# One pair of heads prepared in the stage before, a second one early, and both scan directions inverted in lockstep

## The chip, the cores and the metric

The kernel runs on one core of one Trainium2 chip. The metric is the time of one execution on the device in microseconds (us). Three runs of the kernel before gave 1978.81, 1972.71 and 1967.83 us, so its median is 1972.71 us.

## What is computed

One inference step of a two-layer flow-matching backbone with 1024 channels. There are 384 tokens: 128 context tokens and 256 latent tokens on a grid 64 wide. Everything is in 32-bit floats. Each layer does this:

```python
h = rmsnorm(x) * (1 + sc1) + sh1                   # sc, sh, gt: "modulation", silu(cond) @ ada_w + ada_b
x = x + 0.5 * gt1 * (silu(h @ Wg) * (h @ Wu)) @ Wo # feed-forward, 2816 hidden
p = (rmsnorm(x) * (1 + sc2) + sh2) @ mix_w_in      # one projection for three mixers
o = concat(gla(p_gla), hyena(p_hy), rwkv7(p_rw))   # 6 heads | FFT long convolution | 6 heads
x = x + gt2 * (o @ mix_w_out)
x = x + 0.5 * gt3 * feed_forward(...)
```

The RWKV-7 mixer runs in both directions along the tokens. For each head and direction the state follows `state = state * w_t + (state @ a_t) b_t^T + v_t k_t^T`, and the output is `state @ r_t`. GLA is a chunked gated linear attention, also in both directions. The final states of the context tokens are outputs too.

## The kernel before

Tokens lie along the free dimension and channels on the 128 partitions. A program (`with nc.Block()`) is written per stage and runs one instruction list per engine, in exactly the order in which the Python calls it; there is no planner. Semaphores order the engines: each `..._step` raises one, each `after_...` waits for it. A wait blocks everything behind it on its engine. The stages of a layer are `ffn_stage`, `mix_in_stage`, `mixers_stage` and a second `ffn_stage`.

`mix_in_stage` makes the 13 units of `mix_w_in`, each 48 products of 128x386 in three passes, streamed through two weight slots, and computes the Hyena mixer beside them. `mixers_stage` does GLA and RWKV-7. RWKV's six heads go as three pairs, called A, B and C (pairs 0, 1 and 2); one head sits on partitions 0 to 63 and the other on 64 to 127 (`half(e)`). The methods of class `Pair` are the steps of a pair:

- Preparation: low-rank products (`pe_low`), sigmoids, decay sums by a scan (`dve_decay_sums`), unit keys with their root, inverse and spread (`pe_gate_norm`, `pe_spread_k`), then gate, turned values and bonus, the decayed keys (`dve_decayed`, 5 instructions per direction), the products `nat` and six `gram` products.
- Inverse: in 64-token chunks a triangular matrix is inverted by powers, in ten dependent steps s1, s2, s2q, s3, s4, s5, s6, s7, s8, s9. In the kernel before each step is a call per direction z, for example `pe_s4(pe, 0)` and `pe_s4(pe, 1)`. `each` issues 12 products of 64x64, alternating between the array's quadrant for head 0 (partitions 0 to 63 in and out) and the one for head 1. A product appears as two MATMUL instructions in the trace. PE's result of a direction is evicted by ACT or DVE (`act_inverse`, `dve_power_q`, `dve_q`, `dve_y`), and then that direction's next product may start.
- Scan: four dependent steps of `x`, `u`, `state` and `out`, then a normalisation (`pe_mean`, `pe_var`, `pe_spread_v`, `dve_out`).

Each pair holds three PSUM banks for itself and shares bank 6; bank 7 is for the modulation. Pair C reuses the memory and the banks of pair A and so is begun when A's output is written (`after_first_pair`). Pair B uses GLA's banks and is begun when GLA ends (`after_gla`). The order in `mixers_stage` is: A's preparation and inverse beside GLA, then A's scan beside B's preparation, then B's inverse beside C's preparation, C's inverse beside B's first scan steps, and both scans.

Between these steps PE works through `ada(pe, s, kt)`: products with the modulation weights, 32 units of 1 MB in layer 0 and 16 in layer 1. They are loaded through two slots in the first half of the stage and three in the second (`ADAS`), by the SP queue.

Of the kernel before, what the change touches and what calls it, by code (L numbers as in the profile page):

```python
# [24 lines left out]
TOK = CTX + LAT  # L25
KT = D_MODEL // 128
C = 64
# [80 lines left out]
def build(nc, x_in, cond, ada_w, ada_b, w1_in, w1_out, mix_in, mix_out, w2_in, w2_out, gains, final_gain, chan, lowrank_a,  # L108
# [15 lines left out]
    with stack:  # L124
# [287 lines left out]

        class Place:
# [4 lines left out]
            def __init__(self, at):  # L418
                self.at = at

            def __call__(self, name, shape, dt=F32):
                names[0] += 1
# [683 lines left out]
        def mix_in_stage(lay, P, PR, TG, AL, MO, buffers, following):  # L1106
# [5 lines left out]
            MIX = Steps(" ".join(f"m{i}_s m{i}" for i in range(N_TILES - N_PLAIN)) + " al_g al_s al")  # L1112
# [7 lines left out]
            with ExitStack() as scope, nc.Block() as block:  # L1120
# [7 lines left out]
                HC = sb(scope, "hyena_const", [128, NHCONST])  # L1128
                HW = sb(scope, "hyena_w", [128, 640])
                UC = sb(scope, "conv", [128, 6, W386])  # L1130
# [4 lines left out]
                XALR = flat_zt[0:32, 0:PADT]  # L1135
                RN = UC[0:HY_HID, 5, 0:TOK]
# [25 lines left out]
                def _(act):  # L1162
# [18 lines left out]
                    for n, u in enumerate(UNITS):  # L1181
# [15 lines left out]
                        if n == 10:  # L1197
# [6 lines left out]
                def _(dve):  # L1204
# [4 lines left out]
                    def tap(i, name, at):  # L1209
                        row = P[:, T_HY + i, at:at + W386]  # L1210
                        if at == 1:
                            op = nc.vector.tensor_scalar(UC[:, i, :], row, chn("conv_w", 6 + i), chn("conv_b", i), ALU.mult, ALU.add)
                        else:
                            op = nc.vector.scalar_tensor_tensor(UC[:, i, :], row, chn("conv_w", 6 * at + i), UC[:, i, :], ALU.mult, ALU.add)
# [60 lines left out]
                    def hyena_out():  # L1275
# [6 lines left out]
                        for ct in range(2):  # L1282
                            for (a, b), x0 in zip(SEGS, seg2(UC[:, ct, :])):
# [39 lines left out]
                    for n in range(N_MIX):  # L1323
# [9 lines left out]
                        if n == 4:  # L1333
                            wait_own("e5")
                            nc.vector.tensor_tensor(Z[:, :, :], UC[:, 2:4, :], UC[:, 4:6, :], ALU.mult).then_inc(hdve_done, DV.step("z"))
                        if n in (9, 10):
                            spectrum(n - 9)
                        if N_HY + 1 <= n <= N_MIXED:
                            dve.wait_ge(pb_done, n)
                            for t in range(2):  # L1340
                                i = 2 * (n - 1 - N_HY) + t
                                if i:
                                    dve.wait_ge(mix_done, 2 * i)
                                shift_mix(dve, PR[:, i, :], 128, i, SH[:, :], SHT[:, :], PR[:, i, 0:TOK], mix_done, MIX, f"m{i}")
                        if n == 11:
                            low_rank_input()
                        if n == 12:
                            hyena_out()
                            evict(n)

                @block.tensor
                def _(pe):
# [55 lines left out]
                    for n, u in enumerate(UNITS):  # L1408
# [36 lines left out]
        class Pair:  # L1445
# [3 lines left out]

            def __init__(self, place, sems, lay, pr, banks, shared, PR, TG, AL, MO, shared_free=None):  # L1450
# [5 lines left out]
                self.PE = Steps("loww low g kk vt kspread bonus nat0 nat1 gram00 gram01 gram02 gram10 gram11 gram12 " +  # L1456
                                " ".join(f"s{i}_{z}" for i in ("1", "2") for z in z2) + " s2q_0 s2q_1 s3_0 s3q_0 s3_1 s3q_1 " +
                                " ".join(f"s{i}_{z}" for i in ("4", "5", "6", "7", "8", "9") for z in z2) + " " +
                                " ".join(f"x{t} u{t} s{t} o{t}" for t in range(3)) + " x3 u3 o3 mu var vspread")
                self.AC = Steps("kx2 sigw siga kt g kstd vt e1 e2 first bt00 bt01 bt02 bt10 bt11 bt12 " +  # L1460
                                " ".join(f"s{i}_{z}" for i in (1, 2, 3, 5, 6) for z in z2) + " u0 u1 u2 u3 o sq std")
                self.DV = Steps("st_init kfloor km rk cum kinv kk bn bon bl ab0 ab1 r d0 et0 d1 et1 mr00 mr01 mr02 mr10 mr11 mr12 " +
                                " ".join(f"s{i}_{z}" for i in ("1", "2q", "3q", "4", "7", "8", "9") for z in z2) + " " +
                                " ".join(f"x{t} u{t} sum{t} st{t}" for t in range(3)) + " x3 u3 oc og vinv on out")
                self.PL = Steps("identity decay q0 q1")
# [1683 lines left out]
```

## Time and profile before

| | us |
|---|---|
| median of three runs | 1972.71 |
| the profiled execution | 1975.78 |
| its span, first to last instruction | 1974.0 |
| PE busy | 1885.5 (96%) |
| DVE busy | 1092.9 (55%) |
| ACT busy | 744.2 (38%) |
| POOL busy | 32.1 (2%) |
| mean granted PE clock | 0.986 of full speed |

PE is TensorE, PEld its weight loads, DVE is VectorE, ACT is ScalarE, POOL is GpSimd, SP issues the DMAs. Matmuls overlap in the pipeline, so PE's busy time is a union of modelled spans. The stretches in the rows below were cut where PE's instructions show a step begin: the mixers' stage of layer 0 runs from 472.45 to 700.87, that of layer 1 from 1429.40 to 1649.17.

### The profile page before, as it was taken

What the parts mean: (1) busy time and instruction counts of PE and PEld (TensorE: products, weight loads), DVE (VectorE), ACT (ScalarE), POOL (GpSimd) and SP (SyncE); (2) the same over time, 40 slices, a digit from 0 to 9 for tenths busy, and PEclk for the clock granted to TensorE, in tenths of its full rate; (3) what the DMA queues carried; (4) which work ended last, traced back from release to release, by engine and by line L of the source; (5) the groups of instructions that cost most, each with busy time, mean ns of one, the idle gap of its engine ahead of it and who ended that gap; (6) DMA issues with size and microseconds to landing.
All of it is one profiled execution on the core that took longest, in us unless ns stands there. A gap on an engine that the chain in (4) does not pass through costs nothing. (4 is left out here: it accounts for less than half of the span.)

```text
span 1974.0 us, 38649 instructions
## 1 busy us (share of the span) xinstructions
PE 1885.5 (96%) x16410; PEld 1739.0 (88%) x16410; DVE 1092.9 (55%) x1853; ACT 744.2 (38%) x1117; POOL 32.1 (2%) x64
## 2 busy tenths in 40 slices
PE   5999999998889999999999999999978899999998
PEld 3988999996666789999999999999947688999997
DVE  3544444865766475555455554477576746655533
ACT  3333333345334254333343333344363324433322
POOL 0000000000001000000000000000000100000000
PEclk9999999998999999999999999999989999999999
DMA  7766233423446343332343333342241412333332
GB/s 280 275 221 220 103 119 136 176 86 93 129 152 219 115 147 128 127 123 100 132 147 128 127 116 108 127 187 95 78 131 49 130 50 87 128 117 119 106 132 91
DMA packets 73335, 263.25 MB, mean 133 GB/s; under 512 B 9712, under 2 KB 11120, under 8 KB 57072
## 3 DMA queue, kind: packets, MB, share of 16 engines
q1 hardware_dynamic: 73200, 261.27, 39.0%
q8 instruction: 107, 1.75, 0.4%
q14 instruction: 28, 0.23, 0.0%
HBM read 259.08 MB, written 2.16 MB: 132 GB/s over the span
## 5 line engine op out<-in xcount | busy, mean ns | idle before, releaser
L160 PE MATMUL ps<-h_head,w_head 128*128 128x386 f32 x1824 | 623.5, 342 | 4.1 <-ACT h_head L293 2.1
L160 PE MATMUL ps<-h_head,w_rest 128*128 128x386 f32 x1824 | 619.3, 340 | 0.0
L160 PE MATMUL ps<-h_rest,w_head 128*128 128x386 f32 x1824 | 617.3, 339 | 0.0
L223 ACT ACTIVATE w_head<-w_raw 128x2048 fp32r<-128x2048 f32 (+1 forms) x176 | 303.0, 1722 | 606.0 <-PE ps L160 588.8
L226 DVE TENSOR_TENSOR w_rest<-w_raw,w_head 128x2048 fp32r<-128x2048 f32 (+1 forms) x176 | 360.6, 2049 | 209.3 <-ACT w_head L223 209.3
L160 PEld LDWEIGHTS ps<-h_head,w_head 128*128 128x128 f32 x1824 | 345.8, 190 | 23.1 <-issue 16.9
L160 PEld LDWEIGHTS ps<-h_head,w_rest 128*128 128x128 f32 x1824 | 345.9, 190 | 0.0
L160 PEld LDWEIGHTS ps<-h_rest,w_head 128*128 128x128 f32 x1824 | 343.0, 188 | 0.2
L160 PE MATMUL ps<-gu_head,w_head 128*128 128x384 f32 x832 | 278.4, 335 | 0.1
L160 PE MATMUL ps<-gu_head,w_rest 128*128 128x384 f32 x832 | 277.7, 334 | 0.0
L160 PE MATMUL ps<-gu_rest,w_head 128*128 128x384 f32 x832 | 277.7, 334 | 0.0
L405 DVE TENSOR_TENSOR gate_in<-ps,rstd_all 128x386 f32<-128x386 f32 x88 | 49.2, 559 | 199.8 <-PE ps L160 199.7
L160 PEld LDWEIGHTS ps<-gu_head,w_head 128*128 128x128 f32 x832 | 156.0, 188 | 1.4 <-issue 0.4
L160 PEld LDWEIGHTS ps<-gu_rest,w_head 128*128 128x128 f32 x832 | 156.0, 188 | 0.1
L160 PEld LDWEIGHTS ps<-gu_head,w_rest 128*128 128x128 f32 x832 | 156.2, 188 | 0.0
L823 ACT ACTIVATE gu_head<-gu 128x384 f32 (+1 forms) x88 | 46.2, 526 | 198.5 <-DVE gu L934 198.5
L686 DVE SCALAR_TENSOR_TENSOR x<-ps,gate,x 128x128 f32<-128x128 f32 (+1 forms) x96 | 34.9, 412 | 107.1 <-PE ps L160 107.1
L939 DVE TENSOR_TENSOR gu_rest<-gu,gu_head 128x384 f32 (+1 forms) x88 | 49.2, 559 | 63.7 <-ACT gu_head L823 63.7
L820 ACT ACTIVATE silu<-gate_in 128x128 f32<-128x128 f32 (+1 forms) x176 | 69.2, 440 | 10.8 <-DVE gate_in L405 10.8
L934 DVE SCALAR_TENSOR_TENSOR gu<-up_in,silu 128x128 f32<-128x128 f32 (+1 forms) x176 | 65.2, 412 | 1.6 <-ACT silu L820 1.6
L160 PE MATMUL ps<-ar_identity,bk 64*64 64x64 f32 (+1 forms) x576 | 46.2, 293 | 17.6 <-ACT bk_tok L1810 12.9
L160 PEld LDWEIGHTS ps<-ar_identity,bk 64*64 64x64 f32 (+1 forms) x576 | 34.0, 168 | 32.4 <-ACT bk_tok L1810 21.7
(300 smaller groups left out, 1784.2 us busy)
## 6 DMA issues: line engine op xcount, KB each, us to landing
w_raw<-in_w_in SPq DMA_DIRECT2D x88, 1024.0 KB, 4.8
w_raw<-in_w_out SPq DMA_DIRECT2D x64, 704.0 KB, 4.1
w_raw<-in_ada_w SPq DMA_DIRECT2D x41, 1024.0 KB, 6.3
ada_raw<-in_ada_w SPq DMA_DIRECT2D x31, 1024.0 KB, 6.3
w_raw<-in_mix_in SPq DMA_DIRECT2D x26, 1024.0 KB, 4.8
w_raw<-in_mix_out SPq DMA_DIRECT2D x8, 1024.0 KB, 5.0
hyena_const<-in_hconst SPq DMA_DIRECT2D x2, 1792.0 KB, 9.4
x<-in_x_in SPq DMA_DIRECT2D x1, 1536.0 KB, 12.1
```

The costliest lines, as they stand in the source:

```text
L160: return nc.tensor.matmul(out, lhsT, rhs, start=start, stop=stop)
L223: return nc.scalar.activation(self.HI[src], self.RAW[src], ACT.Copy)
L226: return nc.vector.tensor_tensor(self.LO[src], self.RAW[src], self.HI[src].bitcast(F32), ALU.subtract)
L405: return nc.vector.tensor_tensor(out, bank(b, WIDE), self.ALL[:, :], ALU.mult)
L686: last = nc.vector.scalar_tensor_tensor(xs, psum[:, a:b], g, xs, ALU.mult, ALU.add)
L820: last_silu = nc.scalar.activation(SIL[:, j, a:b], GRAW[:, j, a:b], ACT.Silu, bias=GRAW[:, j, TOK + s:TOK + s + 1])
L823: nc.scalar.activation(GHI[:, ds(k * 2 + j, 1), :].rearrange("p o t -> p (o t)"), GU[:, j, :], ACT.Copy)\
L934: last_gu = nc.vector.scalar_tensor_tensor(GU[:, j, a:b], URAW[:, j, a:b], URAW[:, j, TOK + s:TOK + s + 1], SIL[:, j, a:b], ALU.add, ALU.mult)
L939: nc.vector.tensor_tensor(GLO[g].rearrange("p o t -> p (o t)"), GU[:, j, :], GHI[g].rearrange("p o t -> p (o t)").bitcast(F32), ALU.subtract)\
```

## The change

**Preparation of pair A in the stage before.** `mix_in_stage` gets A and calls its first part between its last units. The rest of A's preparation (gate, turned values, bonus, decayed keys, nat, gram) stays in `mixers_stage`.

```diff
@@ mix_in_stage, ACT, unit loop
+                        if n == 10:
+                            A.act_square(act)
+                            A.act_decay_rates(act, 0)
+                            A.act_decay_rates(act, 1)
                         evict(n, u)
+                        if n == 10:
+                            A.act_key_rate(act)
+                            A.act_key_factor(act)
+                            A.act_decays(act)
+                            A.act_key_root(act)
...
-                        if n == 10:
+                        if n == 9:
                             wg = T_WG - N_PLAIN
@@ DVE
+                        if n == 6:
+                            low_rank_input()
                         if n == 11:
-                            low_rank_input()
+                            A.dve_decay_sums(dve)
+                            A.dve_keys(dve)
+                            A.dve_key_floor(dve)
                         if n == 12:
+                            A.dve_key_inverse(dve)
                             hyena_out()
+                            A.dve_unit_keys(dve)
+                            A.dve_rates(dve)
                             evict(n)
@@ PE
                             signal_back()
+                            pe.wait_ge(low_done, 1)
+                            A.pe_decay_rank(pe, 0)
+                            A.pe_decay_rank(pe, 1)
...
+                                if (n, t, kt) == (11, 0, 5):
+                                    A.pe_key_rank(pe)
+                                if (n, t, kt) == (11, 1, 0):
+                                    A.pe_norm(pe)
+                                if (n, t, kt) == (12, 0, 6):
+                                    A.pe_spread_k(pe)
```

Buffers get new addresses for this (`Homes`), so that A's tiles, and later C's, do not overlap what is still in use.

**Pair C early on one bank.** C's low-rank products, sums and unit keys run through bank 6 alone during A's scan, beside B's preparation. Its gate, values, bonus, decayed keys, nat and gram follow after A's end.

```diff
+                        C.in_banks(6, 6, 6, 6)
+                        after_first_inverse(pe)
+                        C.pe_decay_rank(pe, 0)
...
+                        after_first_pair(pe)
+                        C.in_banks(0, 1, 2, 0)
+                        C.pe_gate(pe)
+                        C.pe_turn_v(pe)
+                        C.pe_bonus(pe)
```

**Lockstep on four quadrants.** A step of the inverse is now one call for both directions. It issues 24 products in which direction 0 uses the quadrants (0 to 0) and (1 to 1) and direction 1 uses (0 to 1) and (1 to 0), and it waits for the evictions of both directions first. Because direction 1's result lands in the other half of the partitions, its steps on DVE that combine it with data in the old half are written as two instructions over 64 partitions (in `dve_nat` the off-diagonal part, in `dve_power_q`, `dve_q` and `dve_y` all of direction 1), and so is its `pool_q`.

```diff
+            def pe_s4(self, pe):
+                self.both(pe, self.after_act, "s3")
+                self.both(pe, self.after_dve, "s3q")
+                self.each(self.second_banks(), self.of(self.D8, self.far), self.q_far, "s4", (0, 0))
...
+            def each(...):
+                for c in range(NCH):
+                    for e in range(2):
+                        for z in range(2):
+                            last = mm(bank(banks[z], TOK)[half(to[z] ^ e), c * C:c * C + C], lhsT(z, c, e), rhs(z, c, e))
...
@@ dve_y
+                if z == 0:
+                    last = nc.vector.tensor_tensor(self.Y[:, 0, :, :], self.XQ[:, 0, :, 1, :], product, ALU.add)
+                else:
+                    for e in range(2):
+                        last = nc.vector.tensor_tensor(self.Y[half(e), 1, :, :], self.QB[half(e)], product[half(1 - e)], ALU.add)
```

**New orders.** Each engine's list in `mixers_stage` is rewritten, one list for layer 0 and one for layer 1. In PE's list for layer 0 the part that follows A's end now alternates B's inverse with C's gram, and C's inverse with B's last inverse steps and B's scan:

```diff
+                        B.pe_s1(pe)
+                        ada(pe, 2, 5)
+                        C.pe_gram(pe, 0, 0)
+                        B.pe_s2(pe)
+                        C.pe_gram(pe, 0, 1)
+                        B.pe_s2q(pe)
...
+                        C.pe_s1(pe)
+                        B.pe_s789(pe, 7)
+                        ada(pe, 3, 1)
+                        C.pe_s2(pe)
+                        B.pe_s789(pe, 8)
+                        C.pe_s2q(pe)
+                        B.pe_s789(pe, 9)
```

The `ada` units are spread anew: in layer 0, units 7 to 12 now stand in A's inverse where one stood before. All of them go through two slots; the three-slot second half is gone, and SP's list loads units 2 to 15, then 16 to 19 after GLA, then 20 to 31 after A's end, with the state loads and stores between.

## Rows read from the trace of the kernel before

**Rows 1.** First line of the page.

```profile
span 1974.0 us, 38649 instructions
```

**Rows 2.** Busy by stretch: length, PE, PEld, DVE, ACT, POOL, clock, DMA share, GB/s.

```profile
472.45:521.21 48.76, 38.55 (x456) 20.59 (x456) 32.18 (x59) 30.19 (x42) 6.03 (x11) 0.82 0.44 134
521.21:557.53 36.32, 33.63 (x912) 30.59 (x909) 22.97 (x72) 7.57 (x13) 0.00 (x0) 1.00 0.30 92
557.53:602.38 44.85, 39.51 (x613) 24.19 (x611) 29.02 (x65) 23.32 (x46) 6.37 (x12) 1.00 0.66 205
602.38:667.38 65.00, 62.48 (x1527) 51.81 (x1523) 38.08 (x76) 19.10 (x42) 2.56 (x6) 1.00 0.45 141
667.38:700.87 33.49, 29.87 (x535) 20.54 (x531) 15.53 (x43) 8.02 (x25) 0.00 (x0) 1.00 0.61 194
1429.40:1476.32 46.92, 35.75 (x455) 20.12 (x456) 32.37 (x59) 30.07 (x42) 5.93 (x11) 0.89 0.46 140
1476.32:1513.33 37.01, 33.81 (x904) 31.79 (x901) 22.97 (x73) 7.57 (x13) 0.00 (x0) 0.95 0.21 62
1513.33:1557.84 44.51, 35.36 (x553) 25.01 (x551) 29.16 (x65) 22.84 (x45) 6.49 (x12) 0.92 0.15 40
1557.84:1619.54 61.70, 60.27 (x1511) 51.29 (x1507) 37.74 (x75) 18.83 (x41) 2.56 (x6) 1.00 0.35 115
1619.54:1649.17 29.63, 26.44 (x478) 21.73 (x479) 15.74 (x44) 7.81 (x26) 0.00 (x0) 0.88 0.03 6
385.00:470.50 85.50, 85.50 (x473) 82.53 (x471) 54.56 (x92) 32.07 (x48) 0.00 (x0) 1.00 0.26 87
```

**Rows 3.** Timeline of PE in the first inverse: start, us, instruction.

```profile
516.05 2.75 PE L160 MATMUL ps<-mixer_out,k_tok 64*32 64x64 f32 x144
...
518.73 0.92 PE L160 MATMUL ps<-ar_identity,bk 64*128 64x192 f32 x8
...
527.25 2.82 PE L160 MATMUL ps<-power_and_q,decay_inv 64*64 64x128 f32 x48
...
543.39 3.01 PE L160 MATMUL ps<-decay_in,chunk_start_state 32*64 32x64 f32 x144
...
546.33 1.61 PE L160 MATMUL ps<-power,decay_incl 64*64 64x64 f32 x48
...
547.88 1.06 PE L160 MATMUL ps<-w_raw,cond_silu 128*32 128x512 f32 x8
```

**Rows 4.** Timeline of DVE and ACT in the first inverse.

```profile
524.27 0.49 ACT L1816 ACTIVATE decay_inv<-ps 128x384 f32<-128x384 f32 x1 [0.91 <-PE ps L160]
...
530.38 0.34 DVE L1941 TENSOR_TENSOR power_and_q<-power_and_q,ps 128x192 f32<-128x192 f32 x1
...
532.57 0.54 DVE L1846 TENSOR_TENSOR power_and_q<-power_and_q,ps 128x384 f32<-128x384 f32 x1
```

**Rows 5.** Timeline of DVE in the mixers' opening, layer 0.

```profile
476.04 1.67 DVE L2248 TENSOR_SCALAR decay_in<-ps,chan 128x386 f32<-128x386 f32 x3 [2.97 <-PE ps L160]
...
482.47 0.95 DVE L1863 TENSOR_TENSOR_SCAN cum<-const,sig_w 128x384 f32<-128x384 f32 x1
...
489.92 2.06 DVE L1896 TENSOR_TENSOR bk<-power_and_q,decay_inv 64x384 f32<-64x384 f32 x4
...
498.70 2.62 DVE L2254 SCALAR_TENSOR_TENSOR decay_in<-decay_in,exp 128x772 f32<-128x772 f32 x2
```

**Rows 6.** Timeline of ACT and PE in the opening, layers 0 and 1.

```profile
493.14 0.83 ACT L2199 ACTIVATE exp<-exp 64x772 f32<-64x772 f32 x1
...
475.93 3.64 PE L160 MATMUL ps<-w_raw,cond_silu 128*32 128x512 f32 x16
...
1431.69 1.92 PE L160 MATMUL ps<-w_raw,cond_silu 128*32 128x512 f32 x16
```

**Rows 7.** PE at the start of pair 1: three low-rank products' first two.

```profile
558.75 0.91 PE L160 MATMUL ps<-p_rwkv,lowrank_w 32*128 32x384 f32 x4
```

**Rows 8.** DMA issues of the modulation weights: count, KB each, median us to landing.

```profile
w_raw<-in_ada_w SPq DMA_DIRECT2D x41, 1024.0 KB, 6.3
```

More of the change, by code:

```diff
@@ L1445, in build @@
         class Pair:
+            EARLY = ("loww0 loww low kk kspread".split(), "kx2 sig0 sigw siga kt e1 e2 kstd".split(), "cum km rk kfloor kinv kk bn".split())
             def __init__(self, place, sems, lay, pr, banks, shared, PR, TG, AL, MO, shared_free=None):
@@ new lines, in both, with near, far, of @@
+            def both(self, pe, after, *names):
+                for name in names:
+                    for z in range(2):
+                        after(pe, f"{name}{z}" if name == "q" else f"{name}_{z}")
+            def near(self, z, e):
+                return half(e)
+            def far(self, z, e):
+                return half(e ^ z)
+            def of(self, buf, side):
+                return lambda z, c, e: buf[side(z, e), z, c, :]
+            def power(self, side):
+                return lambda z, c, e: self.XQ[side(z, e), z, c, 0, :]
@@ L1946, in dve_q @@
                 self.after_pe(dve, f"s{i}_{z}")
-                self.tt(self.XQ[:, z, :, 1, :], self.XQ[:, z, :, 1, :], bank(bb, TOK).rearrange("p (c t) -> p c t", t=C), ALU.add, f"s{i}_{z}")
+                product = bank(bb, TOK).rearrange("p (c t) -> p c t", t=C)
+                if z == 0:
+                    last = nc.vector.tensor_tensor(self.XQ[:, 0, :, 1, :], self.XQ[:, 0, :, 1, :], product, ALU.add)
+                else:
+                    old, new = (self.QB, self.XQ[:, 1, :, 1, :]) if i == "3q" else (self.XQ[:, 1, :, 1, :], self.QB)
+                    for e in range(2):
+                        last = nc.vector.tensor_tensor(new[half(e)], old[half(1 - e)], product[half(e)], ALU.add)
+                self.dve_step(last, f"s{i}_{z}")
             def dve_y(self, dve, i, z):
@@ new lines, in mixers_stage @@
+                LEFT, RIGHT = Place(homes.above), Place(homes.right_at)
+                G = Gla(Place(0, decay_in=LEFT, exp=LEFT, exp_cum=LEFT, exp_minus_cum=LEFT, cum=LEFT, std=LEFT, chunk_start_state=RIGHT, score=RIGHT, k_tok=RIGHT),
+                        SEMS[5:10], lay, (3, 4, 5), P, MO)
+                row_at = LEFT.at
+                mod_row = LEFT("mod_row", [128, 1, 2, ADA_W // 2])
+                A.begin_late(SEMS[0:5])
+                A.in_banks(0, 1, 2, 6)
+                late_at = homes.outer().at
@@ new lines, in mixers_stage @@
+                assert homes.ceiling <= nc.sbuf_top and LEFT.at <= homes.early_at and RIGHT.at <= late_at
+                B_ROWS, B_LEFT, B_RIGHT = Place(homes.rows_at), Place(homes.above), Place(homes.right_at)
+                B = Pair(Place(0, gram=B_ROWS, bonus=B_ROWS, ar_identity=B_LEFT, bk=B_LEFT, bk_tok=B_LEFT, uv=B_LEFT, state_t=B_LEFT, chunk_decay=B_LEFT, power4=B_LEFT,
+                               power_and_q=B_RIGHT, sig_w=B_RIGHT, cum=B_RIGHT, decay_incl=B_RIGHT, decay_inv=B_RIGHT),
+                         SEMS[15:20], lay, 1, (3, 4, 5), 6, PR, TG, AL, MO)
@@ new lines, in mixers_stage @@
+                assert B_ROWS.at <= homes.hyena_rows and B_LEFT.at <= row_at
+                C_SUMS, C_BONUS = Place(B_RIGHT.at), Place(homes.above - 4 * TOK)
+                C = Pair(homes.outer(cum=C_SUMS, bonus=C_BONUS), SEMS[20:25], lay, 2, (6, 6, 6), 6, PR, TG, AL, MO)
+                assert C_SUMS.at <= late_at and C_BONUS.at <= homes.above and homes.hyena_rows + 4 * 6 * TOK <= homes.above - 4 * TOK
+                B.shared_free, C.shared_free = (C.dve_done, C.DV["kk"]), (B.act_done, B.AC["s6_1"])
@@ L2360, in mixers_stage @@
+                ADA = Ada(None, SEMS[10:15], 2, [7] * sets, 1, None, mod_row)
                 bias_done = SEMS[25]
                 def ada(pe, s, kt):
[L2363 to L2367 removed]
+                    if s < sets:
+                        if s and kt == 0:
+                            pe.wait_ge(bias_done, s)
+                        ADA.products(pe, 1)
```

1723 lines of the change are left out of this document (1079 added, 644 removed).

## The prediction, made before the changed kernel was timed

> **What bounds the kernel now.** I read the page, then busy time by stretch, then the timelines of PE, DVE and ACT in the mixers' stage. The span is 1974.0 us [rows 1]. Of it 228.4 us and 219.8 us are the two mixers' stages, which the change rewrites; the rest is dense products, where PE has no gap (85.50 of 85.50 us busy in the last row of [rows 2]). I split each mixers' stage at marks of PE into five stretches, in the order of the first ten rows of [rows 2]: the opening (to A's s1), A's inverse, A's scan with B's preparation, the inverses of B and C, and the tail. Layer 0 has 48.8, 36.3, 44.9, 65.0 and 33.5 us, layer 1 has 46.9, 37.0, 44.5, 61.7 and 29.6. The reader is to see two kinds. In the inverses of B and C PE is busy 62.48 of 65.00 us: only less work on PE, or a better filling, shortens them. In the opening PE is busy 38.55 of 48.76 at a clock of 0.82: there a chain over DVE and ACT decides. The scan stretch lies between (39.51 of 44.85 for PE, 29.02 for DVE).
>
> **Four quadrants.** A step of 24 products, 48 instructions, took from 546.33 to 547.88, 1.55 us, on two quadrants [rows 3]; two calls less one change of shape take about 1.4. Four 64x64 quadrants at once are not in the trace. From below: 48 at the rate of the 64*32 products (144 from 516.05 to 518.73, 18.6 ns each, on four column tiles) are 0.89 us; the 32*64 ones (144 from 543.39 to 546.33, 20.4 ns) give 0.98 [rows 3]. From above: no gain, 1.4; more work than before it is not. I take 0.95, as both neighbours spread over four tiles, so 0.45 saved. Between s1 and s9 there are 11 such groups of 48 per pair (s1 and s3 have two), and s2q, 48 instructions of 64x128 in 2.82 us, which I take to 1.4. That is 11 x 0.45 + 1.4 = 6.4 us per pair, 38 for six.
>
> The two row halves of a direction write one bank. Their instructions of 64 columns follow every 32 ns, 0.50 ns a column, and s2q's take 0.46; the modulation's products on four column tiles of full height take 1.06 us for 8 x 512 columns, 0.26 ns a column, half of that [rows 3]. So in this trace two quadrants seem to run at once although they share a bank. By the rule of the Trainium skill (TensorEngine Tiling, section Gotcha 1: PSUM Pressure), different row tiles cannot access the same PSUM bank at once. If that bound the new steps, only two quadrants, one for each bank, could work at a time, and nothing of the 38 us would come; rival 1 below has this result from the rows. The trace so far speaks against it.
>
> **What lockstep costs.** Before, one direction's eviction lay under the other's product. Now PE waits for both. An eviction is 0.49 us on ACT and 0.54 on DVE [rows 4]; direction 1's DVE steps become two of 64 partitions, and such an instruction costs the same as a full one (4 of 64x384 in 2.06 us, 0.51 each [rows 5]). With 0.3 for the hand-over on both sides (an estimate: 0.2 after the product, 0.1 after the eviction), a step takes 0.95 + 0.3 + 0.98 = 2.2 us when ACT evicts, 0.95 + 0.3 + 0.54 + 1.05 = 2.85 when DVE does, and s2q with its eviction (direction 1 in pieces of 0.34 us [rows 4]) 4.6. The ten steps of a lone pair are then s1 3.1, s2 2.2, s2q 4.6, s3 3.1, s4 2.85, s5 and s6 2.2 each, s7 to s9 2.85 each: 28.8 us, of which PE works 12. So the saving is worth something only where other work fills PE.
>
> **Opening.** In layer 0 GLA's `dve_log_decay` starts at 498.70 [rows 5], 26.2 after the stage, and all behind it (scans, gram, turned keys, states) follows as a chain to s1. ACT had its logarithm ready at 493.97 [rows 6]; DVE came late, behind A's preparation. After: DVE has low keys and init 0.5, decayed keys 5.2 (ten instructions at about 0.52), `decay_in` 1.67 + 0.5 [rows 5], and at 0.54 to 0.6 per instruction of 384 columns [rows 4] receptance 1.0, bonus 1.2, nat 3.6: 13.7 in all. ACT gets `decay_in` at 8.0 and needs 7.5 for abs, exp and logarithm (six instructions of 0.83 [rows 6]) and two table loads: 15.5. So the chain starts 10.7 earlier with PE at full speed. PE's part before nat (GLA's decay products, gate, values, bonus, two `ada` units) is about 12 us at half speed, and its nats 5 more (16 instructions took 3.64 us in layer 0, 1.92 in layer 1, where PE had its 2.4 GHz [rows 6]), which puts the chain's start at 19: 7 earlier. I take 7 in layer 0 and 10 in layer 1: -17.
>
> **Cost in the stage before.** PE is full there, so A's part counts whole: three low-rank products 0.75 [rows 7] + 0.74, key sums 0.35, spread 0.85, and four interruptions of a run at 0.2: 3.4 us per layer, +7 for two. DVE's 54.56 and ACT's 32.07 of 85.50 us [rows 2] hide theirs. ACT's split of the last unit's weights now stands behind two sigmoids that wait for PE: 2.5 + 1.7, and DVE's 2.0 after it, ends 6.4 us into a unit of 8.5, so it stays hidden; without that cover it would be 1 to 3 us per layer. `pe_spread_k` stands 3.2 us into unit 12, its inverse is ready after some 2.
>
> **A's inverse.** Walking the lists: the chain of 28.8, GLA's within and between products (7 us, of which 5.7 exposed between s5 and s6), and scores and outputs that stand in DVE's queue before the pair's evictions (some 3): 37.5. PE saves 6.4 and gets it back as waiting; layer 0 also does five more `ada` units here, 1.0 us each, mostly inside those waits. 36.3 becomes 38, 37.0 becomes 37.5: +2.2.
>
> **A's scan.** PE gets C's early part and nat (8 us) and gives one `ada`. DVE's 29.02 us [rows 2] grow by C's: sums 1.9 (0.95 each [rows 5]), keys, inverse, unit keys and rates 3.4, bonus 1.2, decayed 5.2, receptance 1.0, nat 3.6: 45 us before B's s1 can start. Walked through, A's output comes at about 36 to 38 after the start of its scan, then C's gate, bonus and decayed keys take 12 more until B's s1. I take 50 and 49 for 44.9 and 44.5: +9.7.
>
> **Inverses of B and C.** C's preparation and nat (5.7 us of PE) are gone from here, and 12.8 are saved on quadrants. PE's work falls from 62.5 to about 43. Chain: from B's s1 to the end of C's s1 24.3 us, in which C's gram and `ada` fill all but 3; then C's other nine steps beside B's s7 to s9 and the first steps of its scan 28.2, where DVE, with up to 3.1 for C's s2q, is the late one. That is 52.5 for 65.0. In layer 1, with three `ada` units fewer, 49.5 for 61.7: -24.7.
>
> **Tail.** B's scan is a step further when C's begins, so the tail is C's own chain, 19 us, some `ada`, and the normalisation, 9 to 10: 29 for 33.5 and 28 for 29.6: -6.
>
> **DMA.** Each `ada` unit is 1 MB, 6.3 us from issue to landing [rows 8]. With two slots a unit is ready 6.3 after the use of the one two before. Over 200 us for 32 units this distance is 12, so I cost it at nothing; the pairs of units 3 to 4 us apart are where it could show. SP's stores and state loads stand between, but behind events that PE's own order also waits for.
>
> **Sum.** -17 + 7 + 2.2 + 9.7 - 24.7 - 6 = -28.8, so -29. Against the profiled execution's 1975.78 this is 1947. The median of the runs is 3 lower, so I name 1944. Bounds: quadrants at no gain take back about 32 (most of the 38 stands in filled stretches once the product is no faster); the opening between 5 and 12 per layer; the scan stretch between no loss and 9 per layer.
>
> **Rivals.**
> 1. Quadrants do not overlap. For it: nothing in the trace has the four 64x64 quadrants at once. Against it: the two neighbours of [rows 3] with four tiles. Time: 1944 + 32 = 1976, about what there was.
> 2. Lockstep waits decide, and it is slower. Place: each of 60 steps (ten, three pairs, two layers), where PE waits for the later of two evictions which itself queues behind another pair's work on DVE. The sum has 29 us to give; from 0.5 us more per step than I walked it turns, at 0.7 it gives 1944 + 42 = 1986. For it: DVE's load in the scan and B/C stretches rises to 75 to 90%. Against it: gram, `ada` and the other pair stand between nearly all steps.
> 3. The two slots starve PE: 18 units in the later halves waiting 1 us each leave 1962. For it: 6.3 us per landing. Against it: the spacing.
> 4. The waits are filled better than I walked. Then PE's savings come whole: 38 + 17 - 7, and some of the idle time goes: 1920.
>
> **Chances.** Forecast 0.50 (1930 to 1960), rival 1 0.10, rival 2 0.12, rival 3 0.08, rival 4 0.20. What a measurement can tell from no change is about 0.5%, 10 us: faster means under 1963, slower over 1982. Faster: the forecast, rival 4 and half of rival 3, 0.74. Same: the other half, rival 1 and a little of rival 2, 0.15. Slower: the rest of rival 2, 0.11. The range of 8 in 10 holds rival 1 and leaves out rival 2 and the far side of rival 4: 1908 to 1978.
>
> **What would show it.** Right: 48 instructions of a lockstep step in 0.9 to 1.0 us; A's s1 38 to 41 us after the mixers' stage begins; `mix_in_stage` 3 to 4 us longer; B's s1 to C's scan in 50 to 54 us. Wrong: 1.4 us for a step (rival 1); gaps of PE ended by DVE's cum or power_and_q of over 1 us at most steps (rival 2); gaps ended by DMA of w_raw (rival 3); PE busy over 95% in the B and C stretch (rival 4).

## The result, and the profile after

The changed kernel takes 2001.3 us (median of 4, 1996.8 to 2004.1) where the kernel before takes 1970.3 (median of 4). It is slower: the ratio is 1.0151, with a 95% interval of 1.0123 to 1.0179. The forecast was 1944, in a range of 1908 to 1978.

The first row of the profile after, then busy time by stretch at the same marks as [rows 2]: the five stretches of the mixers' stage in layer 0, the five in layer 1, and one of dense products.

```profile
span 2001.4 us, 38754 instructions
```

```profile
476.10:517.39 41.29, 34.13 (x420) 18.54 (x420) 28.53 (x53) 22.49 (x31) 6.97 (x12) 0.79 0.49 157
517.39:562.74 45.35, 35.44 (x962) 26.11 (x959) 27.62 (x80) 10.45 (x18) 1.95 (x3) 0.92 0.54 166
562.74:619.22 56.48, 48.75 (x708) 31.66 (x712) 42.01 (x87) 25.38 (x52) 7.24 (x15) 0.88 0.47 137
619.22:684.22 65.00, 49.70 (x1491) 36.10 (x1487) 34.30 (x69) 12.29 (x31) 2.76 (x3) 0.92 0.48 147
684.22:714.17 29.95, 25.83 (x435) 19.57 (x435) 14.49 (x41) 6.77 (x24) 0.00 (x0) 0.94 0.36 113
1446.31:1495.24 48.93, 39.46 (x419) 20.59 (x419) 30.07 (x61) 22.50 (x31) 7.06 (x12) 0.71 0.44 134
1495.24:1537.64 42.40, 33.78 (x922) 28.42 (x921) 26.05 (x72) 10.11 (x18) 1.95 (x3) 0.81 0.04 8
1537.64:1590.53 52.89, 43.01 (x663) 29.97 (x666) 40.96 (x86) 26.39 (x52) 5.99 (x14) 0.87 0.28 86
1590.53:1649.77 59.24, 44.57 (x1458) 35.42 (x1454) 34.32 (x69) 12.40 (x31) 3.03 (x3) 0.91 0.34 108
1649.77:1676.93 27.16, 23.34 (x417) 18.66 (x415) 14.55 (x40) 6.16 (x23) 0.00 (x0) 0.94 0.02 5
```

The two stages now have 238.1 and 230.6 us, 468.7 in all, against 448.2: 20.5 more. The stages before them grew by 3.6 and 3.6. With the 20.5 that is 27.7 for the span's 27.4, so nothing else moved. Of the 20.5, PE's busy time gives 17.6 back (378.0 for 395.7) and its idle time takes 38.1 (90.7 for 52.5). The clock fell: PE stood at its lower level, 1.2 GHz, for 122.9 us of the two stages, against 44.4 before, by the list of granted clock. So PE's busy time holds much work at half speed, and would have fallen further without it.

PE's own timeline, layer 0 (start, us, instruction; in brackets the idle time before it and what ended it):

```profile
517.39 0.57 PE L160 MATMUL ps<-sig_w,power_and_q 64*64 64x64 f32 x23
520.36 0.58 PE L160 MATMUL ps<-sig_w,power_and_q 64*64 64x64 f32 x25 [2.40 <-issue]
...
521.73 1.93 PE L160 MATMUL ps<-w_raw,cond_silu 128*32 128x512 f32 x8
...
635.76 0.91 PE L160 MATMUL ps<-power_and_q,decay_inv 64*64 64x64 f32 x45
640.05 0.33 PE L160 MATMUL ps<-power_and_q,decay_inv 64*64 64x64 f32 x3 [3.38 <-issue]
```

A step does run in 0.9 us. But it breaks off after 23 of its 48 instructions, in the middle of a step, where nothing is waited for, and goes on 2.40 us later; at 635.76 it breaks off after 45. Then the modulation's products take 1.93 us instead of 1.06: half clock. Such breaks are PE's largest wait now. The waits in layer 0's stage (total, times, longest), after and then before:

```profile
PE ps L160 <- issue: 17.4, 10, 3.4
PE ps L160 <- ACT bk_tok L1927: 7.0, 4, 3.2
PE ps L160 <- DVE sig_w L2069: 4.3, 3, 2.2
```

```profile
PE ps L160 <- issue: 5.4, 6, 1.8
```

With layer 1 (9.3 and 2.8) the "issue" time is 26.7 us for 8.2. What ends in DVE or ACT grew by 20.1 (60.7 for 40.6), all of it in the stretches of the inverses (23.5 for 3.4). The two make up the idle time. Nine of the 21 stretches at half clock stand right behind a break, the others behind waits that DVE, ACT or the start of the stage ended; before, one of nine stood behind a break. The break at 636.67, then a stretch that begins 0.8 us behind its end, and the next:

```profile
636.67:640.05 3.38, 0.00 (x1) 0.00 (x1) 0.00 (x0) 0.00 (x0) 0.00 (x0) 1.00 0.93 261
640.80:644.20 3.40, 3.40 (x60) 2.52 (x58) 2.00 (x5) 0.49 (x2) 0.00 (x0) 0.50 0.11 38
644.20:647.60 3.40, 3.23 (x97) 2.02 (x101) 0.69 (x1) 1.94 (x5) 0.00 (x0) 0.99 0.00 0
```

PE did nothing in the first, worked all of the second at a clock of 0.50, and has 0.99 in the third.

### The profile page after: what moved, and what is told of

It is laid out like the page before. It is cut to its first block and busy times, and to the rows that moved or that the text cites. A ratio compares the mean times of both kernels' runs of the same rounds, so it can differ in the third digit from the quotient of the medians.

```text
span 2001.4 us, 38754 instructions
## 1 busy us (share of the span) xinstructions
PE 1875.5 (94%) x16410; PEld 1708.8 (85%) x16410; DVE 1119.9 (56%) x1899; ACT 738.3 (37%) x1114; POOL 39.1 (2%) x70
## 5 line engine op out<-in xcount | busy, mean ns | idle before, releaser
L160 PE MATMUL ps<-ar_identity,bk 64*128 64x192 f32 (+1 forms) x576 | 51.5, 318 | 23.0 <-ACT bk_tok L1927 16.9
L160 PEld LDWEIGHTS ps<-ar_identity,bk 64*128 64x128 f32 (+1 forms) x576 | 38.4, 185 | 39.8 <-ACT bk_tok L1927 25.7
```

What stands on the lines that cost most here:

```text
L160: return nc.tensor.matmul(out, lhsT, rhs, start=start, stop=stop)
```

## Experiments

Theories. S: PE runs out of instructions, since a step now goes through them faster than they come. D: the loads of modulation weights delay them. K: idle time of any kind halves the clock, and that is a large part. L: lockstep's waits for evictions. Q: the quadrants give all of my 38 us, and the loss is elsewhere. All kernels are the changed one with one edit, if nothing else is said; us is the median, the ratio is to the kernel before (1970 to 1973 in each group). "Issue" and "half" are us of both mixers' stages in the profiled run: PE's waits that end with "issue", and time at 1.2 GHz. The profiled runs of e3, e4, e14 and e18 are 4 to 6 us under their kernels' medians.

| run | us | ratio, 95% interval | issue | half |
|---|---|---|---|---|
| before | 1971 | 1 | 8.2 | 44 |
| changed | 2001 | 1.0151 (1.0123 to 1.0179) | 26.7 | 123 |
| e1 two quadrants | 2016 | 1.0225 (1.0198 to 1.0252) | 13.8 | 82 |
| e2 wide second | 1973 | 0.9999 (0.998 to 1.0019) | 8.3 | 72 |
| e3 quiet loads | 1964 | 0.9957 (0.9937 to 0.9977) | 5.4 | 58 |
| e4 whole evictions | 1988 | 1.0093 (1.0063 to 1.0123) | 29.0 | 89 |
| e5 quiet, kernel before | 1965 | 0.9963 (0.9946 to 0.998) | 1.4 | 44 |
| e6 quiet, two quadrants | 1995 | 1.0117 (1.0093 to 1.0141) | 1.8 | 58 |
| e8 held clock | 1987 | 1.0077 (1.0054 to 1.01) | 17.3 | 75 |
| e9 quarter loads | 2000 | 1.0142 (1.0122 to 1.0163) | 4.1 | 99 |
| e10 quarter, held | 2014 | 1.0203 (1.0173 to 1.0233) | 6.8 | 116 |
| e11 quiet, held, whole | 1960 | 0.994 (0.9924 to 0.9957) | 8.8 | 58 |
| e12 late first | 2016 | 1.0231 (1.0182 to 1.028) | 28.6 | 130 |
| e13 late third | 2037 | 1.0331 (1.0302 to 1.036) | 22.8 | 157 |
| e14 quiet, wide | 1962 | 0.9953 (0.9934 to 0.9971) | 0.0 | 61 |
| e15 unlocked | 1988 | 1.0084 (1.0064 to 1.0103) | 16.1 | 72 |
| e16 unlocked, held | 1989 | 1.0084 (1.0061 to 1.0107) | 10.0 | 55 |
| e17 plain inverse | 1989 | 1.0084 (1.0068 to 1.0099) | 9.0 | 65 |
| e18 plain, held | 1987 | 1.009 (1.0062 to 1.0118) | 2.6 | 44 |

**e1, two quadrants.**

```diff
-    for e in range(2):
-        for z in range(2):
-            last = mm(bank(banks[z], TOK)[half(to[z] ^ e), ...
+    for z in range(2):
+        for e in range(2):
+            last = mm(bank(banks[z], TOK)[half(to[z] ^ e ^ z), ...
```

> The changed kernel (2001 us), but direction 1's products are put on the two quadrants that direction 0 uses, so its results land in the other half and are not the reference's. Lockstep, order and number of instructions stay. A step of 48 instructions should take 1.4 to 1.55 us instead of 0.9. Theory S (PE runs out of instructions: 26.7 us of PE's idle time in the two mixers' stages end with 'issue', by something that comes in blocks, when PE works through instructions faster than they arrive): the slower step needs no faster supply, the 'issue' time falls to 8 us or less and the half clock behind it goes with it, so the time rises by 0 to 12 us only, 2001 to 2013. Rival Q (the quadrants give all of the 38 us that I priced, and the loss is elsewhere): 2026 to 2039. Rival L (PE waits for evictions at each step, its own time is hidden): within 4 us of 2001, with 'issue' as it was.

2016, 14 us more, between S and Q. The breaks halved, and half clock fell with them, though not to the level of before. So four quadrants are worth 14 us here, not 38.

**e2, wide second.** (The same for s2q.)

```diff
+    if z and c and (c, e) != (NCH - 1, 1):
+        continue
+    if z and not c:   # all six chunks' columns against chunk 0's stationary side
+        last = mm(bank(banks[1], TOK)[half(to[1] ^ e), :]..., lhsT(1, 0, e), rhs(1, slice(0, NCH), e))
```

> The changed kernel, but direction 1's six products of 64 columns per half are one product of 384 columns (s2q: two), plus one of 64 at the end of the step, so a step has 30 instructions for 48 at the same columns; direction 1's results are not the reference's. Four quadrants, waits and evictions stay. Theory S (supply of instructions): the 'issue' time in the two mixers' stages falls from 26.7 us to under 12, half clock falls with it, and the time by 15 to 30 us, to 1971 to 1986. Rival L (lockstep's waits for DVE and ACT): PE's step is no shorter, so 1996 to 2004. Rival K (the clock alone, from idle time of any kind): also 1996 to 2004.

1973, 28 less: S, against L and K. The waits for DVE and ACT are the same (62.5 us for 60.7) and so are the columns but for one product more; the number of MATMULs, and of weight loads with them, fell (7868 to 6596 in the two stages). That fewer instructions are no gain in themselves is seen in e14. In layer 0:

```profile
PE ps L160 <- issue: 4.6, 4, 1.3
```

**e3, quiet loads.**

```diff
+    rows = slice(0, 128 if self.loaded is None else 8)
-    sp.dma_start(self.RAW[...], ada_slice(first, u))
+    sp.dma_start(self.RAW[...][rows], ada_slice(first, u)[rows])
```

> The changed kernel, but in the mixers' stages each load of the modulation's weights (1 MB) brings only 8 of 128 partitions, with the same semaphores; the modulation is wrong by that. Theory D (the instruction blocks of PE wait on the DMA engines behind these loads): the 'issue' time falls from 26.7 us to under 10 and the time by 12 to 25 us, to 1976 to 1989. Against it (the blocks need their time whatever else is moved): 'issue' over 20 us, the time within 4 us of 2001. Starved slots (my rival 3) would show here too: the 0.6 us that PE waits for w_raw go, no more.

1964, 38 less, more than D's 12 to 25. The breaks went (2.0 and 3.4 us). The same stretches in layer 0, and the opening and the inverses of B and C in layer 1:

```profile
476.08:517.18 41.10, 33.80 (x419) 18.44 (x419) 28.51 (x53) 22.50 (x31) 6.97 (x12) 0.79 0.06 16
517.18:555.74 38.56, 32.92 (x962) 24.82 (x959) 27.47 (x80) 9.24 (x16) 1.54 (x3) 0.96 0.05 15
555.74:607.23 51.49, 43.00 (x703) 27.43 (x706) 41.51 (x87) 26.55 (x54) 7.41 (x15) 1.00 0.06 18
607.23:659.53 52.30, 45.25 (x1494) 32.80 (x1490) 34.52 (x70) 12.19 (x31) 3.02 (x3) 1.00 0.05 14
659.53:686.64 27.11, 23.76 (x435) 17.84 (x435) 14.50 (x41) 6.78 (x24) 0.00 (x0) 1.00 0.26 86
1418.79:1461.15 42.36, 35.29 (x419) 18.61 (x419) 28.65 (x53) 22.51 (x31) 7.06 (x12) 0.76 0.05 15
...
1553.02:1605.61 52.59, 41.96 (x1462) 33.30 (x1458) 34.43 (x69) 12.40 (x31) 3.00 (x3) 0.97 0.14 48
```

A's inverse has 38.6 us for 45.4, and the inverses of B and C 52.3 for 65.0, at a clock of 1.00 for 0.92. By the two profiled runs the stages are 45.7 us shorter: the breaks give 21.3, PE's busy time for the same instructions gives 29.5 (348.5 for 378.0, with 65 us less at half clock), and the waits for DVE and ACT take 5.0 back.

**e4, whole evictions.**

```diff
-    for e in range(2):
-        last = nc.vector.tensor_tensor(new[half(e)], old[half(1 - e)], product[half(e)], ALU.add)
+    last = nc.vector.tensor_tensor(new, old, product, ALU.add)
```

> The changed kernel, but direction 1's evictions on DVE in the inverse are one instruction of 128 partitions instead of two of 64 that also swap halves (results of direction 1 wrong). DVE does some 3.7 us less for each pair, 22 in all. Rival L (lockstep's waits decide: each DVE step is 0.5 us shorter and PE waits for it): 10 to 20 us less, 1981 to 1991. Theory S: the waits for evictions are small beside the stalls, 2 to 6 us less, 1995 to 1999.

1988, 14 less, with the breaks as they were: L has a part of its own. The waits for DVE and ACT fell by 10.8 us (49.9 for 60.7), and half clock by 34.

**e5 and e6.** e3's edit on the kernel before (its third slot is loaded in full once in each layer), and e3's with e1's.

> The kernel before (1972), with the same cut of the modulation's loads in the mixers' stages as in the run with quiet loads (8 of 128 partitions; modulation wrong). The changed kernel fell from 2001 to 1964 by it. Theory D+S (loads delay PE's instructions, and the new inverse, which uses instructions 1.5 times as fast, pays far more): the kernel before has 8 us of 'issue' to lose and little half clock behind it, so 3 to 12 us less, 1960 to 1969; the changed kernel is then level or ahead only when the loads are quiet. Rival (the loads cost every kernel alike, by ports or landings): 1930 to 1940.

> The changed kernel with both cuts: quiet loads (1964 alone) and direction 1 on direction 0's quadrants (2016 alone). It prices the four quadrants when instructions arrive freely. If my 38 us of PE time were right and come through: 1996 to 2002. If lockstep's waits cover most of a shorter step (rival L): 1975 to 1988. With loads on, the difference was 14.

1965 and 1995. The loads cost the kernel before 7 us and the changed one 38. So quiet against quiet, the change is worth 1 us (1965 to 1964), and not 29. Four quadrants are worth 31 us when loads are quiet (1995 to 1964), 14 when they are not. My account of PE's time was about right, and loads took half of it. And with quiet loads as well, the changed kernel on two quadrants is 30 over the one before.

**e7, supply run.** Behind all outputs of each mixers' stage, with no wait between:

```diff
+    for four in (True, False):
+        for _ in range(20):
+            for c in range(NCH):
+                for z in range(2):
+                    for e in range(2):
+                        mm(bank((6 if four else 4) + z, TOK)[half(e ^ z if four else e), ...], ident half, heads half)
```

> The changed kernel with a run of products without waits at the end of each mixers' stage, after all its outputs: 20 steps of 48 instructions of 64x64 on four quadrants (960 instructions and their weight loads), then 20 on two. In layer 0 no load is in flight; in layer 1 SyncE keeps two loads of 1 MB in flight meanwhile. At the rate of the steps in the kernel they take 18 us and 29 us. Theory S+D: in layer 0 18 to 24 and 29; in layer 1 the four quadrants take as long as the blocks of instructions need, 3.5 us or more for 128 products with weights, so 26 to 35 us, with breaks that end with 'issue'. Rival (supply is not delayed by loads): the same times in both layers. The time of the whole says nothing (about 50 + 60 us more).

(Run once; its time as a whole says nothing.)

PE, layer 0, no load in flight:

```profile
701.57 2.10 PE L160 MATMUL ps<-const 64*64 64x64 f32 x128 [1.37 <-issue]
705.03 2.10 PE L160 MATMUL ps<-const 64*64 64x64 f32 x128 [1.37 <-issue]
708.49 2.10 PE L160 MATMUL ps<-const 64*64 64x64 f32 x128 [1.37 <-issue]
```

DMA queues in 697 to 719:

```profile
q8 instruction: 6, 0.10, 1.7%
```

Layer 1, two loads in flight, first four quadrants, then two:

```profile
1733.67 2.10 PE L160 MATMUL ps<-const 64*64 64x64 f32 x128 [3.23 <-issue]
1739.88 10.19 PE L160 MATMUL ps<-const 64*64 64x64 f32 x256 [4.12 <-issue]
1751.50 3.95 PE L160 MATMUL ps<-const 64*64 64x64 f32 x128 [1.43 <-issue]
1756.34 3.83 PE L160 MATMUL ps<-const 64*64 64x64 f32 x124 [0.90 <-issue]
```

This is the cause laid bare. In layer 0 PE did the first 270 MATMULs without a break. From there on it stops after every 128, which with their weight loads are 256 instructions; one packet of 16 KB on the queue "instruction" belongs to each such block, 64 bytes an instruction. Four quadrants go through a block in 2.10 us, and the next is there 3.46 us after the last, though no load runs: 27 ns a MATMUL. Two quadrants need 3.95 us a block and run without a break in layer 0. With 1 MB loads in flight the distance is 6.2 us (1733.67 to 1739.88) and 4.8 (1751.50 to 1756.34), and 3.7 to 6.2 over all of them, so two quadrants break off too. In layer 0 four quadrants took 25.6 us and two 28.6, in layer 1 37.5 and 41.9: S and D hold, and both delays are longer than I expected. The loads of this run are heavier (319 GB/s over 1733 to 1785) than those of the changed kernel (146 in layer 0's stage).

The Trainium skill (Runtime: NRT & Kernel Launch, section Instruction fetch mechanics) has the blocks of 256 instructions, and the trace agrees. It also says that the fetch is hidden since instructions are issued more slowly than they arrive. Here they are issued faster: 2.10 us for a block that takes 3.46 to come.

**e8, held clock.** 17 such units in all, where PE waited 1 to 3.2 us:

```diff
+    for j in range(4):   # weights of zero, added into the open sums of bank 7
+        mm(bank(7, ADA_W, 32 * j, 32 * j + 32), cst("ident", 0, 32, 64, 128), cst("scan", 0, 512, 64, 128), False, False)
```

> The changed kernel plus products with weights of zero into the open sums of bank 7 (nothing changes in the values), 8 instructions of 512 columns or 1.06 us each, at places where PE waited 1 to 3.2 us: 9 in layer 0 (5 in the opening), 8 in the opening of layer 1. Theory K (idle time of PE halves its clock, and that is a large part of the loss): the openings' clock rises from 0.79 and 0.71 to over 0.9, half clock falls by 25 us or more, and the time by 6 to 15 us, 1986 to 1995. Rival (in the openings a chain over DVE and ACT decides, and PE's clock is hidden): the clock rises, the time stays within 4 us of 2001 or rises.

1987, 14 less, and half clock fell by 48 us: K's sizes, though PE has 18 us more to do. But not in K's place. The openings, where 13 of the 17 units stand, were to rise over 0.9 and have 0.78:

```profile
477.38:523.74 46.36, 41.70 (x460) 21.71 (x460) 29.57 (x61) 22.49 (x31) 6.97 (x12) 0.78 0.46 142
1436.63:1484.09 47.46, 44.29 (x483) 20.43 (x483) 28.57 (x53) 22.51 (x31) 7.05 (x12) 0.78 0.45 138
```

With 46.4 and 47.5 us for 41.3 and 48.9 they are longer together. The gain comes behind them, where the breaks fell too (26.7 to 17.3 us in all), so the 14 us are not the clock's alone.

**e9 and e10.** Each load in four parts of 32 partitions, at most two parts in flight; e10 with e8's edit as well.

```diff
+    for q in range(4):
+        if self.last_quarter: sp.wait_ge(*self.last_quarter)
+        sp.dma_start(self.RAW[...][32 * q:32 * q + 32], ...).then_inc(full[q % 2], 16)
```

> The changed kernel (2001), but each 1 MB load of the modulation's weights in the mixers' stages goes out as four loads of 32 partitions, of which SyncE keeps at most two in flight (0.5 MB at most for up to 2 MB before). The same bytes move. Theory D1 (PE's blocks of instructions queue behind the bytes already waiting on the DMA engines): the 'issue' time falls from 26.7 us to 12 to 18 and the time by 8 to 20 us, 1981 to 1993. Rival D2 (it is the moving itself, or units that now land later): 'issue' stays over 22 us; 1998 to 2010.

> The changed kernel with both edits that leave its results as they are: quarter loads, and the products with zero weights in PE's waits (1987 alone). If both causes are real and mostly apart: 1968 to 1980, level with the kernel before (1972). If quarter loads do nothing: 1985 to 1990.

2000 and 2014. In e9 the breaks went from 26.7 to 4.1 us, more than D1 had, and the time stayed: the weights now come late. In e10 the products with zero weights, a gain of 14 us in e8, cost 14, against both of my cases; why is open. PE's waits in e9, whole span:

```profile
PE ps L160 <- DMA w_raw<-in_ada_w: 44.8, 26, 4.5
PE ps L160 <- DMA ada_raw<-in_ada_w: 17.2, 7, 8.1
...
PE ps L160 <- issue: 4.1, 3, 1.9
```

Whether the short queue or the slower pace ended the breaks is not settled.

**e11 and e14.** e11 is e3's, e4's and e8's edits together, e14 e2's and e3's.

> The changed kernel with three cuts together: quiet loads (-38 alone), products with zero weights in PE's waits (-14 alone) and direction 1's evictions in one instruction (-14 alone); modulation and direction 1 wrong. It asks whether these three are what my forecast of 1944 lacked. If they add up: 1936. Since half clock behind stalls falls by the first as well as by the second, I expect some overlap, 1938 to 1952. If over 1955, a fourth cause is open.

> The changed kernel with two cuts: quiet loads (1964 alone, -38) and direction 1's products made wide, 30 instructions a step for 48 (1973 alone, -28). Theory S (both take away the same thing, PE waiting for its instructions, and the half clock behind it): 1956 to 1964, little under the better one. If they are two causes they add up: 1932 to 1942.

1960 and 1962. Fewer instructions (-28) and quiet loads (-38) together give -39: they take away the same thing. And e14 is level with e3: once loads are quiet, 1272 fewer MATMULs gain 1 us, so their worth in e2 was the supply. Held clock and whole evictions, 14 each alone, give 4 together once loads are quiet (1964 to 1960), less than my range for e11 had. Either the breaks made most of what they cured, or the zero weights cost here what whole evictions gain: half clock is 58 us in e3 and e11, the waits for DVE and ACT fell by 19.5 us, and PE has 18 more to do. Quiet loads with whole evictions alone were not run.

**e12 and e13.** Pair 0's, then pair 2's early part moved back. In e13 the order around pair 1's first steps is mine, after the one before.

```diff
-    A.pe_decay_rank(pe, 0) ... A.pe_spread_k(pe)      # mix_in_stage; ACT and DVE likewise
+    A.pe_decay_rank(pe, 0) ... A.pe_spread_k(pe)      # opening of mixers_stage
```

```diff
-    C.in_banks(6, 6, 6, 6) ... C.pe_spread_k(pe)      # in A's scan
+    C.pe_decay_rank(pe, 0) ... C.pe_spread_k(pe)      # behind after_first_pair, on banks 0, 1, 2
```

> The changed kernel (2001), with pair 0's early part (decay rates, keys, their inverse roots, spread) back at the start of the mixers' stage and out of the stage before; all else stays. By my working the part moved saves 7 and 10 us of the openings and costs 3.4 in each stage before, so 10 us are lost: 2011. By the trace of the changed kernel layer 0's opening gained 7.5, layer 1's lost 2, and each stage before grew by 3.5, so undoing it costs nothing: 1996 to 2004.

> The changed kernel, with pair 2's early part behind pair 0's end, on banks 0 to 2, between pair 1's last gram and its first steps as in the kernel before. By my working this part costs 9.7 us in pair 0's scan and gives 10 to 15 in the inverses of pairs 1 and 2, so undoing it: 2001 to 2008. If DVE's load in the scan is a loss that the inverses don't pay back (their time goes by stalls and evictions): 1985 to 1996.

2016 and 2037: both early parts pay within the changed kernel, by 15 us (10 by my working) and by up to 35. Neither of my cases for e13 had that side. How much of the 35 is my order is open.

**e15 to e18.** e15 issues each step direction by direction; e17 has the old layout and quadrants too; e16 and e18 add e8's edit.

```diff
     def pe_s2(self, pe):
-        self.both(pe, self.after_act, "s1")
-        self.both(pe, self.after_dve, "s1")
-        self.each(self.first_banks(), ..., "s2", (0, 0))
+        for z in range(2):
+            self.own(pe, self.after_act, "s1", z)
+            self.own(pe, self.after_dve, "s1", z)
+            self.each(self.first_banks(), ..., "s2", (0, 0), z)
```

```diff
     def far(self, z, e):
-        return half(e ^ z)
+        return half(e)        # e17: nor half(to[z] ^ e); evictions whole, et1 and q1 in one piece
```

> The changed kernel (2001) with the same layouts, banks, halves and order lists, but each step of an inverse first waits for direction 0 and issues its 12 products (two quadrants at a time), then the same for direction 1; so one direction's eviction lies under the other's product, as in the kernel before, and 48 instructions take about 1.4 us again. Results stay as they are. If lockstep is the loss (its waits, its bursts of instructions, the half clock behind both): 'issue' falls from 26.7 us to under 14 and the time to 1965 to 1985. If the four quadrants' speed is worth its 14 us and lockstep costs nothing: 2010 to 2018, like the run on two quadrants in lockstep (2016).

> The same without lockstep, plus the products with zero weights in PE's waits (14 us less when alone with the changed kernel). Results stay as they are. If PE's clock is still a loss there: 5 to 12 us under the run without lockstep; if the waits that they fill have gone, 0 to 8 over it.

> The changed kernel with the inverse as it was before (each direction by itself, its own halves, two quadrants, whole evictions), and pair 0 and pair 2 early as changed, in the changed order lists, with two slots for the loads. Results stay as they are. If the third part of the change is all of the loss, and the other two gain something as their undoing says (14 and 35 us in the changed kernel): under 1968, faster than both. If the new order lists, made for lockstep, or the two slots, hold the rest: 1972 to 1984.

> The same plus the products with zero weights in PE's waits. With lockstep gone they gave nothing (1989 to 1988). The waits in the openings are as long here, so by theory K 3 to 8 us under the run without them; by that result, within 3 us of it.

1988, 1989, 1989 and 1987, all four slower than before by 0.8 to 0.9%; e15 lies 3 us and e17 5 above the ranges that I had. Lockstep costs 28 us (e1 to e15), four quadrants give half of it back. Without it the waits for DVE and ACT are 41.7 us (e15), as before the change (40.6). The swapped halves cost nothing once the directions go by themselves (e17 to e15). What stays, 17 us, is the frame: the two early parts, two slots and the new order lists; no run parts them. In e17's profile 7.6 of its 12.3 us over the kernel before are the stages before, and most of the rest is layer 1's stage (224.3 for 219.8). No kernel that keeps its results beat the one before.

## Why the prediction was wrong

By its steps, in layer 0 and layer 1:

| step | forecast | changed | quiet (e3) |
|---|---|---|---|
| opening | 41.8, 36.9 | 41.3, 48.9 | 41.1, 42.4 |
| A's inverse | 38, 37.5 | 45.4, 42.4 | 38.6, 39.4 |
| A's scan | 50, 49 | 56.5, 52.9 | 51.5, 52.5 |
| B and C | 52.5, 49.5 | 65.0, 59.2 | 52.3, 52.6 |
| tail | 29, 28 | 30.0, 27.2 | 27.1, 25.6 |

**Four quadrants.** Right in size: 0.93 us for 48 instructions, 1.54 for s2q. The 12 instructions that fall to one quadrant are 768 columns in 0.93 us, 1.2 ns each, near the 1.0 ns that a column tile of the modulation's products takes (1024 columns in 1.06 us). Two quadrants taking turns on their bank would need 1.6 us. So all four ran at once and rival 1 falls. The rule of the Trainium skill (TensorEngine Tiling (Array Packing), section Gotcha 1: PSUM Pressure) does not hold for these steps, as two row tiles write different halves of one bank. The step that failed is the next one, that the 38 us count where PE is full: there PE waits for its instructions. e1 measures 14, e6 31. I had the neighbours at 18.6 and 20.4 ns from [rows 3] and took them as a rate that can be kept up. They were bursts of 144, little more than the one block of 128, and breaks of this kind stood in the trace of before, 8.2 us of them. I named "issue" in no sum.

**The inverses of B and C**, the largest term (-24.7), came out at -2.5. In layer 0 it has 11.2 us of breaks, and half clock behind them. With quiet loads layer 0 is at 52.3, within 0.2 of my walk. So close is luck in part: that profile is 6 us under its kernel's median.

**The clock** was the second thing missing. I gave it to the opening alone, and took 1.00 for all else because [rows 2] show it there in layer 0; layer 1 has 0.95, 0.92 and 0.88 in three stretches. The 1.00 belonged to a PE with fewer gaps. I removed work from PE, kept its waits, and left the clock as it was. What it costs alone no run shows: e8's 14 us hold fewer breaks as well, and without lockstep the same products took half clock from 72 to 55 us (e16) and gained nothing.

**Lockstep.** I walked the waits in full clock and without breaks, as 28.8 us for a lone pair, and the quiet kernel shows A's inverse as forecast (38.6). Beside loads lockstep costs 28 us (e1 to e15). Rival 2 had the side right and was given 0.12. Its mechanism, later evictions, makes 20.1 of the 38.1 us of idle time. Over 60 steps that is 0.34 us each, under the 0.5 from which I had it turn the sum by itself. The other half, the breaks, was in no rival.

**Opening.** Layer 0 as forecast; layer 1 is 12 us over. I took full clock for it from [rows 6]; it has 0.71. 6.6 of the 12 go with quiet loads; the rest stays where PE waits for a chain over DVE and ACT at a clock of 0.76.

**The stage before** (+3.4 each): 3.6 and 3.6. **A's scan** (+5.1 and +4.5): +11.6 and +8.4, of which 6.6 and 8.0 stay with quiet loads. **Two slots**, rival 3: 0.6 us waited for weights, so it falls in the changed kernel; with slower landings (e9) it is what decides. **Tail**: right.

So of the 57 us between 1944 and 2001, 38 are the delay of PE's instructions by loads, with what it does to clock and waits; that is shown by e3, and by e2 and e14 from the other side. The baseline gains 7 from quiet loads too, so against it the net is 31, and the other half of the miss stands without the loads: quiet against quiet the change gains 1 us for the 29 forecast. That the quiet profile still comes near my figures is because the baseline's own loss to the loads is gone from it too. It is over them in layer 1, whose stage has 212.4 us for the 200.9 forecast, with 37 us at half clock. How this divides into clock and waits is open.

## What to carry to other kernels

Before making a PE step faster by packing more small products side by side, divide its time by its MATMULs: where more than a hundred or two in a row took under 27 ns each, PE stopped for its next block of instructions, and beside loads of 319 GB/s the limit was mostly 38 to 48 ns. Fewer, wider instructions keep the gain where faster ones lose it. And when work leaves a PE that was full, recompute its clock as well: the nine breaks of 1.1 to 3.4 us each had 3.4 to 6.8 us at half clock behind them. Products with zero weights in the waits are worth a run, not more: they gave 14 us in one kernel, nothing in two, and cost 14 in another.

## What had not been expected of the hardware

- PE's instructions come in blocks of 256 (128 MATMULs with their weight loads), one packet of 16 KB each, 3.46 us apart with idle DMA engines and mostly 4.8 to 6.2 while loads of 319 GB/s run (e7).
- By the packets' records, one takes 0.9 to 1.9 us, and PE goes on 1.2 to 1.6 us after its end (the ten breaks of the changed kernel in layer 0).
- Adding 18 us of useless products made a kernel 14 us faster (e8). With lockstep gone the same products took half clock down by 17 and 21 us and gave nothing (e15 and e16, e17 and e18), so time at half clock alone does not tell what it costs.
